# Expert slots counted per token tile: 32 a tile and expert, four-abreast down tiles and a row-tiled combine in a streaming mixture of experts

## What is computed

```
def hier_moe(h, rg_w, rg_b, re_w, re_b, w_gate, w_up, w_down):
    ...
    comb = (jax.nn.one_hot(g_idx, N_GROUPS, dtype=f32)[:, :, None] * e_w[:, None, :]).astype(t.dtype)
    y = jnp.zeros_like(t)
    for g in range(N_GROUPS):
        a = jnp.einsum('td,edf->tef', t, w_gate[g])
        u = jnp.einsum('td,edf->tef', t, w_up[g])
        hm = jax.nn.silu(a) * u * comb[:, g, :, None]
        y = y + jnp.einsum('tef,efd->td', hm, w_down[g])
    return y.reshape(bsz, seq, d)
...
        h = modulate(rms_norm(x, norm2_g[l]), shift2, scale2)
        y = hier_moe(h, router_group_w[l], router_group_b[l], router_expert_w[l], router_expert_b[l],
                     exp_w_gate[l], exp_w_up[l], exp_w_down[l])
        x = x + gate2[:, None, :] * y
    return rms_norm(x, final_norm_g)
```

## Time and profile before

| | |
|---|---|
| median of 3 runs | 1529.9 us (1526.99 to 1530.2) |
| the profiled execution | 1530.55 us, its span 1528.8 us |
| TensorE matmul busy | 1425.4 us (93%) |
| VectorE, ScalarE, GpSimd busy | 549.1, 160.1, 160.3 us |
| transferred | 565.45 MB, mean 370 GB/s |

### The profile page before, as it was taken

The page is one execution under the profiler, slowest core; times in us unless marked ns, Lnnn a source line. Parts: engine busy times, 40 slices in busy tenths (PEclk is TensorE's granted clock), DMA queues, the critical chain, the costliest instruction groups (busy, mean ns, idle before and its releaser), DMA issues.

```text
span 1528.8 us, 18636 instructions
## 1 busy us (share of the span) xinstructions
PE 1425.4 (93%) x7328; PEld 661.6 (43%) x7328; DVE 549.1 (36%) x942; ACT 160.1 (10%) x254; POOL 160.3 (10%) x112
## 2 busy tenths in 40 slices
PE   4979999999999979999999999999999999999976
PEld 2546777666644433333333333343343343333322
DVE  4233999999577440121121121121121111111103
ACT  3140100100411121000000010010010010000001
POOL 1000039159000035000000000000000000000000
PEclk9789999999999989999999999999999999999999
DMA  9999667469989859999999999999999999999992
GB/s 318 384 388 402 229 220 253 160 233 415 400 306 361 347 200 377 409 421 421 421 422 422 422 422 422 422 422 422 422 422 422 422 422 422 422 422 421 421 421 117
DMA packets 111009, 565.45 MB, mean 370 GB/s; under 512 B 10633, under 2 KB 10817, under 8 KB 52657
## 3 DMA queue, kind: packets, MB, share of 16 engines
q1 hardware_dynamic: 108368, 560.02, 91.1%
q10 hardware_dynamic: 2592, 4.78, 1.0%
HBM read 562.62 MB, written 2.13 MB: 369 GB/s over the span
## 4 chain that ended last, share of the span: by engine, by line
PE 66%; DVE 12%; DMA 9%; issue 6%; PEld 3%; PEldq 1%; ACT 1%; SPq 1%; DVEq 0%; ACTq 0%
PE ps L1009 23%; PE ps L1043 14%; PE ps L977 8%; DMA ring<-in_exp_w_down 8%; PE ps L1063 6%; PE ps L801 4%; DVE arena L1751 3%; DVE arena L1721 2%; PEld ps L890 2%; PE ps L784 2%; PE ps L586 2%; PE ps L641 2%; PE ps L890 1%; DMA ring<-in_w_ada 1%; PE ps L602 1%
## 5 line engine op out<-in xcount | busy, mean ns | idle before, releaser
L1009 PE MATMUL ps<-ring,arena 128*64 128x512 f32 x2008 | 450.7, 593 | 7.6 <-DMA ring<-in_exp_w_up 5.0
L1009 PEld LDWEIGHTS ps<-ring,arena 128*64 128x64 f32 x2008 | 151.9, 137 | 276.7 <-issue 273.1
L1043 PE MATMUL ps<-ring,arena 128*64 128x512 f32 x1024 | 242.9, 601 | 21.5 <-issue 10.6
L801 PE MATMUL ps<-arena,ring 128*128 128x256 f32 x896 | 201.5, 382 | 1.2 <-ACT arena L1285 0.8
L801 PEld LDWEIGHTS ps<-arena,ring 128*128 128x128 f32 x896 | 167.8, 190 | 43.3 <-issue 21.7
L1043 PEld LDWEIGHTS ps<-ring,arena 128*64 128x64 f32 x1024 | 71.6, 137 | 162.8 <-issue 154.4
L1974 DVE TENSOR_TENSOR arena<-arena,ps 128x512 f32<-128x512 f32 x64 | 44.0, 687 | 271.5 <-PE ps L1063 263.0
L977 PE MATMUL ps<-arena 128*64 128x256 f32 x1024 | 123.7, 386 | 6.5 <-issue 3.9
L1466 POOL TENSOR_SCALAR skip<-ident,vT 128x128 f32<-128x128 f32 x8 | 98.8, 12349 | 206.7 <-PE ps L851 204.1
L1948 DVE TENSOR_SCALAR arena<-ps,mod 128x256 f32<-128x256 f32 x64 | 34.8, 544 | 227.2 <-PE ps L977 227.2
L890 PE MATMUL ps<-ring,arena 128*128 128x512 f32 x256 | 113.0, 600 | 2.4 <-DVE arena L1782 2.3
(11 more groups left out here) (268 smaller groups left out, 786.5 us busy)
## 6 DMA issues: line engine op xcount, KB each, us to landing
ring<-in_exp_w_down SPq DMA_DIRECT2D x128, 1024.0 KB, 20.7
ring<-in_exp_w_gate SPq DMA_DIRECT2D x127, 1024.0 KB, 18.1
ring<-in_exp_w_up SPq DMA_DIRECT2D x124, 1024.0 KB, 17.1
ring<-in_w_ada SPq DMA_DIRECT2D x96, 1024.0 KB, 14.1
ring<-in_w_in SPq DMA_DIRECT2D x32, 1024.0 KB, 10.5
ring<-in_w_out SPq DMA_DIRECT2D x16, 1024.0 KB, 13.8
arena<-in_exp_w_up SPq DMA_DIRECT2D x4, 1024.0 KB, 11.2
arena<-in_x SPq DMA_DIRECT2D x2, 1024.0 KB, 7.0
```

The costliest lines, as they stand in the source:

```text
L801: last = mm(ps[:, j // 2, (j % 2) * T:(j % 2 + 1) * T], ring[:, s, kk * N + j * P:kk * N + (j + 1) * P], hT[:, k, :], start=(k == 0 and j ...
L1009: last = mm(ps[64 * x:64 * x + 64, stage, :], xT[:, k, slot:slot + SLOTS], unit[:, kk * N:(kk + 1) * N], start=(k == 0), stop=(k == KD - 1 ...
L1043: last = mm(ps[half, 2 + n, :], hidT[pr][:, u, half], job_unit(m + x, False)[:, n * N:(n + 1) * N], start=(u == 0), stop=(u == 3), skip_gr ...
```

## The change

A slot now belongs to an expert and a token tile: 32 slots for each, so a job still has 256. The rank of a token is counted within its own tile, and a block of four experts gets a second job when an expert has more than 32 tokens in one tile. Since a slot takes its token from one tile alone, `gather` no longer adds two tiles into one result but writes each tile's 128 slots by itself, half the columns for each matmul. `down` works with 32 rows for each expert and tile, four abreast, and writes them so that the rows of tile 0 come to stand in partitions 0 to 63 and those of tile 1 in 64 to 127. So `combine` needs for a token tile only 64 rows of `yexp`: its matmuls are 64 rows by 128 columns, one for each tile, beside each other, into two banks. `combine_last` is dropped; the last job uses `combine` too, with other banks. The final variances, roots and scalings of both tiles stand behind the last add, and ScalarE loads its table for the square root ahead of the final squares.

```
-            mm(ps[:, 2, EXP:2 * EXP], before, sel[:, 1, 2, :], start=True, stop=False)
-            mm(ps[:, 2, EXP:2 * EXP], ones, sel[:, 0, 2, :], start=False, stop=True)
-            mm(ps[:, 2, 2 * EXP:3 * EXP], ones, sel[:, 0, 2, :], start=True, stop=False)
-            mm(ps[:, 2, 2 * EXP:3 * EXP], ones, sel[:, 1, 2, :], start=False, stop=True).then_inc(rank_done, 1)
+            mm(ps[:, 2, EXP:2 * EXP], before, sel[:, 1, 2, :], start=True, stop=True)
+            mm(ps[:, 2, 2 * EXP:3 * EXP], ones, sel[:, 0, 2, :], start=True, stop=True)
+            mm(ps[:, 2, 3 * EXP:4 * EXP], ones, sel[:, 1, 2, :], start=True, stop=True).then_inc(rank_done, 1)
...
     def gather(j, i):
+                chosen = pick.rearrange("p (r t x s) -> p r t x s", r=2, t=TT, x=2)
...
-                            last = mm(ps[half, 6 + k % 2, 0:T], x1p[:, t, k, half], pick[:, t, :], start=(t == 0),
-                                      stop=(t == 1), skip_group_check=True)
+                            dst = ps[half, 6 + k % 2, 0:T].rearrange("p (r x t s) -> p r x t s", r=2, x=2, t=TT)
+                            last = mm(dst[:, :, :, t, :], x1p[:, t, k, half], chosen[:, :, t, :, :], start=True, stop=True,
+                                      skip_group_check=True)
...
     def down(j, pr, u):
-                    for x in range(2):
-                        half = slice(64 * x, 64 * x + 64)
-                        last = mm(ps[half, 2 + n, :], hidT[pr][:, u, half],
-                                  job_unit(m + x, False)[:, n * N:(n + 1) * N], start=(u == 0), stop=(u == 3),
-                                  skip_group_check=True)
+                    for t in range(TT):
+                        for x in range(2):
+                            src, dst = 64 * x + 32 * t, 64 * t + 32 * x
+                            last = mm(ps[dst:dst + 32, 2 + n, :], hidT[pr][:, u, src:src + 32],
+                                      job_unit(m + x, False)[:, n * N:(n + 1) * N], start=(u == 0), stop=(u == 3),
+                                      skip_group_check=True)
...
+            def combine(j, n, banks):
+                if n == 0:
+                    pe.wait_ge(scatter_ready, j + 1)
+                if n >= 2:
+                    pe.wait_ge(added, j * 8 + 2 * n - 2)
                 for pr in range(2):
-                    for x in range(2):
-                        last = mm(ps[64 * x:64 * x + 64, 6 + t, :], wpickT[:, pr, t * P + 64 * x:t * P + 64 * x + 64],
-                                  yexp[pr][:, n, :], start=(pr == 0), stop=(pr == 1), skip_group_check=True)
+                    for t in range(TT):
+                        rows = slice(64 * t, 64 * t + 64)
+                        last = mm(ps[:, banks[n % 2] + t, :], wpickT[rows, pr, :], yexp[pr][rows, n, :], start=(pr == 0),
+                                  stop=(pr == 1), skip_group_check=True)
...
-                    if i < 8:
-                        combine(j, i)
+                    if i < 8 and i % 2 == 0:
+                        combine(j, i // 2, SUM_BANKS)
...
-            for i in range(8):
-                combine_last(j_last, i)
+            for n in range(4):
+                pe.wait_ge(down_stored, j_last * 8 + 4 + n + 1)
+                combine(j_last, n, LAST_SUM_BANKS)
...
-                    link(gp_.tensor_scalar(over, counts, float(r * SLOTS), None, ALU.is_gt))
+                    link(gp_.tensor_scalar(over, counts, float(r * HALF_SLOTS), None, ALU.is_gt))
...
-            V.tensor_copy(counts, ps[:, 2, 2 * EXP:3 * EXP]).then_inc(counts_ready, 1)
+            V.tensor_reduce(counts, ps[:, 2, 2 * EXP:4 * EXP].rearrange("p (t e) -> p e t", t=TT), AX.X,
+                            ALU.max).then_inc(counts_ready, 1)
...
-            each = [P, TT * BE, SLOTS]
+            each = [P, TT * BE, HALF_SLOTS]
...
-            final_rows(0)
-            final_var(1)
-            final_rows(1)
+            for t in range(TT):
+                final_var(t)
+            for t in range(TT):
+                final_rows(t)
```

More of the change, by code:

```diff
@@ L47 @@
 SLOTS = 64
+HALF_SLOTS = SLOTS // TT
 BE = 4
@@ L405, in trunk @@
         fin_sq = sem("final_squares")
+        root_table = sem("root_table_in")
         fin_var = sem("final_variance")
@@ L1026, in turn_picks @@
                 pe.wait_ge(wpicks_ready, j + 1)
-                for p2 in range(2):
-                    for t in range(TT):
-                        last = tr(ps[:, 6 + p2, t * P:(t + 1) * P], wpick[:, t, p2 * P:(p2 + 1) * P], P)
+                for pr in range(2):
+                    last = tr(ps[:, 6, pr * P:(pr + 1) * P], wpick[:, pr * P:(pr + 1) * P], P)
                 last.then_inc(picks_turned, 1)
@@ L1922, in _, with slots @@
             ranks = rankc.rearrange("p t e -> p (t e)")
-            each = [P, TT * BE, SLOTS]
+            by_pair = ranks.rearrange("p (r t x) -> p r t x", r=2, t=TT)
+            each = [P, TT * BE, HALF_SLOTS]
+            def slots(v):
+                return v.rearrange("p (n s) -> p n s", s=HALF_SLOTS)
             def picks(j, e0, first_rank):
+                block = rank[:, :, bass.ds(e0, BE)].rearrange("p t (r x) -> p r t x", r=2)
                 if first_rank is None:
-                    V.tensor_copy(rankc[:, :, :], rank[:, :, bass.ds(e0, BE)]).then_inc(pick_order, 1)
+                    V.tensor_copy(by_pair, block).then_inc(pick_order, 1)
@@ L1929, in picks @@
                 else:
-                    V.tensor_scalar(rankc[:, :, :], rank[:, :, bass.ds(e0, BE)], first_rank, None,
-                                    ALU.subtract).then_inc(pick_order, 1)
+                    V.tensor_scalar(by_pair, block, first_rank, None, ALU.subtract).then_inc(pick_order, 1)
                 dve.wait_ge(pick_order, j * PICK_STEPS + 1)
-                V.tensor_tensor(onehot, iota[:, 0:SLOTS].unsqueeze(1).to_broadcast(each),
+                V.tensor_tensor(slots(onehot), iota[:, 0:HALF_SLOTS].unsqueeze(1).to_broadcast(each),
@@ L1939, in picks @@
+                weights = comb[:, :, bass.ds(e0, BE)].rearrange("p t (r x) -> p r t x", r=2)
+                V.tensor_copy(by_pair, weights).then_inc(pick_order, 1)
                 dve.wait_ge(pick_order, j * PICK_STEPS + 3)
-                V.tensor_tensor(wpick.rearrange("p t (e s) -> p (t e) s", e=BE), onehot,
-                                ranks.unsqueeze(2).to_broadcast(each), ALU.mult).then_inc(wpicks_ready, 1)
+                V.tensor_tensor(slots(wpick), slots(onehot), ranks.unsqueeze(2).to_broadcast(each),
+                                ALU.mult).then_inc(wpicks_ready, 1)
@@ L1966, in store_picks, with add @@
                 dve.wait_ge(picks_turned, j + 1)
-                V.tensor_copy(wpickT[:, 0, :], ps[:, 6, 0:T]).then_inc(scatter_half, 1)
-                V.tensor_copy(wpickT[:, 1, :], ps[:, 7, 0:T]).then_inc(scatter_ready, 1)
-            def add(j, i, n, t, bank):
+                V.tensor_copy(wpickT.rearrange("p r q -> p (r q)"), ps[:, 6, 0:T]).then_inc(scatter_ready, 1)
+            def add(j, n, t, bank):
                 cc = slice(n * N, (n + 1) * N)
-                dve.wait_ge(combined, j * 16 + 2 * i + 2)
-                V.tensor_tensor(acc[:, t, cc], acc[:, t, cc], ps[:, bank, :], ALU.add).then_inc(added, 1)
+                dve.wait_ge(combined, j * 8 + 2 * n + 2)
+                V.tensor_tensor(acc[:, t, cc], acc[:, t, cc], ps[:, bank + t, :], ALU.add).then_inc(added, 1)
             def job(j, next_picks):
@@ L1982, in job @@
                 for m in range(8):
-                    add(j, m, m // 2, m % 2, 6 + m % 2)
+                    add(j, m // 2, m % 2, SUM_BANKS[m // 2 % 2])
                 dve.wait_ge(added, j * 8 + 8)
```

65 lines of the change are left out of this document (23 added, 42 removed).

## The result

The changed kernel takes 1517.68 us (median of 4 runs, 1516.22 to 1518.9), the kernel before 1530.05 in the same session (1526.99 to 1530.65): ratio 0.9923, 95% interval 0.9906 to 0.994.

What follows compares the result with a forecast made beforehand. Weight transfers at 422 GB/s, 119.3 us a job, were taken as the bound, covering TensorE inside jobs. Head 4.8 plus tail 5.2, 10.0 us off the profiled 1530.55, gives 1520.5; against the median, 1519.8 us, range 1516 to 1526.5.

Steps and rivals of the forecast that it cites:

- (a): Inside the jobs, `gather`: each matmul moves 128 columns, so 13.8 us a job becomes 9, -4.8 us.
- (b): Inside the jobs, `combine`: matmuls as 64-row tiles run two abreast, 13.7 us a job becomes 6.9.
- (c): Inside the jobs, `down`: twice the instructions but four abreast, so 0 us.
- (d): Inside the jobs: the array's shape changes 24 times a job at 0.17 us each, +4.1 us a job.
- (e): Head: the rank matmuls go from five to four, -0.43 us.
- (f): Head: two picks operations before the first gather narrow from 512 to 256 columns, saving 0.5 us.
- (g): Head: the first eight `gather` steps take 6.6 us instead of 8.79, -2.2 us.
- (h): Head: the two later blocks of four `gather` steps take 2.5 us each instead of 3.50, -2.0 us.
- (i): Tail, last `combine`: 1.71 us for each n, two tiles abreast, so the last add starts 6.1 us earlier.
- (j): Tail: both tiles' variances, roots and scalings follow the last add, 7.5 us instead of 6.66, +0.9 us.
- Code that grows by a sixth: TensorE's longer code for a job: instruction loading would need to stall it over 9 us a job to matter.
- the slower rival: Around `down`: TensorE becomes the bound, jobs pass 119.3 us, about 1546 or 1645 us in all; chance 0.08.

Runs made afterwards that it cites:

- a1: Changed kernel with every gather matmul of the first job issued twice; 1521.94 us, ratio 0.995 to the kernel before.
- a2: Changed kernel with every gather matmul of jobs 2 to 8 issued twice; 1516.13 us, ratio 0.9913 to the kernel before.
- a4: Changed kernel with the matmuls of the last job's combine issued twice; 1523.64 us, ratio 0.9973 to the kernel before.
- t1: Changed kernel with the final scaling's left halves moved from VectorE to GpSimd and ScalarE; 1517.31 us, ratio 0.9935 to the kernel before.
- c0_changed_again: The changed kernel measured once more, unedited, in rounds with the kernel before; 1517.66 us, ratio 0.9932 to the kernel before.
- x1_no_branch_pe: Changed kernel without TensorE's branch and loop for a ninth and later jobs; 1515.89 us, ratio 0.9929 to the kernel before.
- a3: Changed kernel with every gather matmul of jobs 2 to 8 issued four times; 1628.89 us, one run.

## Why the prediction was right

The forecast was 1519.8 us for 1517.68. Its account (the jobs are covered, head and tail pay) is what the two traces and four of the runs show: a1 for the head, a2 for the jobs, a4 and t1 for the tail. The sum came out short: 10.0 us forecast, 11.6 in the spans, 1.2 of the difference in the head and 0.4 in the tail.

- *Inside the jobs, worth 0*: shown by the run with doubled gathers. (a) two steps of `gather` took 0.87 to 1.03 us against 1.72 before, near the best case. (b) Row tiles pair: 32 matmuls in 7.19 us. (c) `down` takes 3.57 to 3.64 us for 32. (d) The shape changes were over-sized: in the timeline a `down` and the two gather steps behind it take 4.59 us (1000.50 to 1005.09), which is 0.30 over 3.43 + 0.86, and a `combine` takes 1.92 (904.51 to 906.43), 0.21 over 1.71; so 8 x 0.30 + 4 x 0.21 = 3.2 us a job, 0.10 to 0.15 a change, not 4.1. The job came to 106.4 us by busy time, below the 108 to 113. But the prediction added its terms to 117.75, the spacing of two jobs, which also holds some 2 us in which TensorE isn't busy; by busy time alone it was 115.8 before, so the change took 9.4 us off a job where 7.6 was forecast.

```profile
904.51 1.99 PE L1063 MATMUL ps<-arena 64*128 64x512 f32 x8
906.43 3.65 PE L1012 MATMUL ps<-ring,arena 128*64 128x512 f32 x16
...
1000.50 3.64 PE L1046 MATMUL ps<-ring,arena 128*32 128x512 f32 x32
1004.07 1.09 PE L980 MATMUL ps<-arena 128*64 128x128 f32 x16
1005.09 3.64 PE L1046 MATMUL ps<-ring,arena 128*32 128x512 f32 x32
```

- *Head*, 5.1 for TensorE and 4.8 for the end, measured 5.94 and 6.0. (e) and (f) were right (-0.93). (g) -2.45 for -2.2, (h) -2.56 for -2.0: of a block's four steps the first pair takes 1.28 us (567.66 to 568.94) and the second 0.94, where I had 1.45 for a pair that waits for its reader. These two terms were mis-sized, by 0.8 together.
- *Tail*: -5.6 for -5.2. (i) -6.1 came as computed (the last add starts 7.84 us after `combine`'s start, before 14.02: -6.2). (j) was over-sized: from the last add's start to the end of the last scaling it is 7.21 us (1506.76 to 1513.97), not 7.5, so +0.55 on the 6.66 of before and not +0.9. That the output "follows by 3.2" on the last scaling fits both profiles (3.19 before, 3.23 now), but as a reason it holds for the kernel before alone, where the transfer stood still until that scaling. In the changed kernel the transfer runs through from the first piece on, and in t1 the last scaling was 2.4 us earlier for nothing. That both paths end at the same time in the changed kernel is chance, and the sum didn't depend on telling them apart.
- *The last `down`* should still have waited for its units, near 1495; one that waits for nothing was named as a sign of being wrong. In the profile above it waited for nothing, in c0_changed_again it waited 1.27 us. What the prediction hadn't in view is the stop of 7.6 to 7.9 us at the loop's exit, which both kernels have and behind which TensorE may or may not catch up with the transfers. By the runs it costs between nothing and 1.0 us, so the sign was a poor one, and the account stands.
- *Code that grows by a sixth* stood in the slower rival with "over 9 us a job needed". The runs show such a stop to be real, 6.5 to 6.9 us a pass with a slower clock behind it, and absent here only because the pass is still short enough.

What stays open: where exactly between 810 and 938 matmul instructions the stop sets in, why leaving the branch out removes the stop at the exit, and why the ranks' matmul moves by 5.8 us between executions. That TensorE waits in the stop for instructions being loaded is inferred from the packets, of which one moves within a stop; no row names its releaser.

## What to carry to other kernels

When transfers bound a phase, split a change into what happens before the queue is full, under it, and after the last transfer: here 58 us of TensorE time went under the queue, at least 36 of them worth nothing, while 6 at the head and 6 at the tail counted fully. Before a loop on TensorE is unrolled further or given more and smaller matmuls, look at the instruction queue's packets and at "issue" at the loop's start; free time on the engine doesn't mean that its code may grow. At the end of a program, measure from the first output piece and look for gaps in the transfer behind it: where there is none, speeding up the work on later pieces gains nothing.

## What the runs showed of the hardware

- A loop on TensorE of 588, 682 or 810 matmul instructions a pass ran without a stop (32 to 34 instruction packets in all; from 722 to 1440 us none in q8 with 810, and from 722 to 1460 none with 682); at 938 and 1,066 each pass but the first began with 6.5 to 6.9 us of idleness (89 and 96 packets of 16 KB, 9 or 10 in a pass), whether the added matmuls had 128 or 8 columns.
- Where the loop is left past a branch not taken, TensorE stood 7.5 to 7.9 us in every kernel that has the branch, and not in x1_no_branch_pe.
- After such a stop the granted clock was 0.50 (893 to 897 us in a3), and the next 32 matmul instructions of 512 columns took 4.9 to 6.4 us instead of 3.64. Waits of 1.3 us for a unit, as in each job here, left it at 1.00.
- A change of the array's shape cost 0.10 to 0.15 us. The Trainium skill (TensorEngine Tiling (Array Packing), section Key Properties) says that a mode change drains the engine; the trace agrees that it isn't free, and the cost is a third to a half of the 0.31 us that the prediction estimated for a full drain.
- 2 MB of output in four pieces ended 6.9 to 7.0 us after the first piece's issue in the changed kernel, in both its profiles, in t1_left_half_elsewhere and in a4_last_combine_twice; in eight pieces 7.4 (374 GB/s instead of 407, the DMA engines busy throughout in both).
